# Forty-eight element-wise products of the delta rule's stage move from GpSimd's queue to VectorE's

## The reference, cut to what matters

```python
decay = jnp.exp(jnp.where(incl, gc[..., :, None] - gc[..., None, :], -jnp.inf))
kb = k * beta[..., None]
m = jnp.where(strict, jnp.einsum('bhnid,bhnjd->bhnij', kb, k) * decay, 0.0)
a_mat = m + jnp.eye(CHUNK, dtype=m.dtype)
sol = lax.linalg.triangular_solve(a_mat, rhs, left_side=True, lower=True, unit_diagonal=True)
...
v_new = u_n - jnp.einsum('bhlk,bhkv->bhlv', w_n, state)
state_next = state * jnp.exp(gl_n)[..., None, None] + jnp.einsum('bhlk,bhlv->bhkv', kd_n, v_new)
...
o = (jnp.einsum('bhnld,bhndv->bhnlv', q * jnp.exp(gc)[..., None], states)
     + jnp.einsum('bhnij,bhnjv->bhniv', attn, v_new))
```

## Time and profile before

| What | Value |
|---|---|
| median of the runs | 1362.28 us (3 runs, 1358.44 to 1362.96) |
| the profiled execution | 1358.39 us, span of its trace 1356.6 us |
| PE busy | 1221.3 us, 90% of the span |
| DVE busy | 814.8 us, 60% |
| POOL busy | 172.9 us, 13% |

### The profile page before, as it was taken

The page is one execution under the profiler, slowest core; times in us unless marked ns, Lnnn a source line. Parts: engine busy times, 40 slices in busy tenths (PEclk is TensorE's granted clock), DMA queues, the critical chain, the costliest instruction groups (busy, mean ns, idle before and its releaser), DMA issues.

```text
span 1356.6 us, 14615 instructions
## 1 busy us (share of the span) xinstructions
PE 1221.3 (90%) x5530; PEld 854.2 (63%) x5530; DVE 814.8 (60%) x1017; ACT 607.4 (45%) x777; POOL 172.9 (13%) x180
## 2 busy tenths in 40 slices
PE   4999999869999999898899399999999999999990
PEld 3788876556768778686468265566666666555540
DVE  7787841675344544426574576666666666666636
ACT  6353434633323324113231274566666666666632
POOL 1000250002313213220000001111111111111000
PEclk8999999979999999998899599999999999999995
DMA  6323321012122212201663899999999999999904
GB/s 237 94 87 114 110 62 38 10 32 75 43 63 57 76 40 62 73 21 55 212 241 119 325 321 333 351 397 407 400 401 402 393 395 392 401 401 396 380 8 189
DMA packets 96011, 278.55 MB, mean 205 GB/s; under 512 B 8768, under 2 KB 58560, under 8 KB 70720
## 3 DMA queue, kind: packets, MB, share of 16 engines
q1 hardware_dynamic: 90672, 268.63, 53.3%
q0 software_dynamic: 5120, 8.40, 1.9%
q10 hardware_dynamic: 144, 0.52, 0.1%
HBM read 267.04 MB, written 18.87 MB: 211 GB/s over the span
## 4 chain that ended last, share of the span: by engine, by line
PE 46%; DVE 2%; DMA 2%; issue 1%; ACT 1%; POOLq 0%; DVEq 0%; SPq 0%
PE yb L1792 17%; PE hb L1764 9%; PE hb L1765 9%; PE hb L1998 2%; PE tx L1748 2%; PE hb L1981 2%; PE gb L1779 1%; PE gb L1772 1%; PE yb L1998 1%; DMA h_dram<-h 1%; DMA xg<-h_dram,rows_all 1%; PE tx L2018 1%; PE yb L1981 1%; DVE yr L2342 0%; DVE h L2332 0%
## 5 line engine op out<-in xcount | busy, mean ns | idle before, releaser
L1881 DVE TENSOR_TENSOR wlo<-wraw,whi 128x2048 fp32r<-128x2048 f32 x127 | 285.4, 2287 | 29.3 <-ACT whi L1824 29.3
L1824 ACT ACTIVATE whi<-wraw 128x2048 fp32r<-128x2048 f32 x128 | 240.9, 1908 | 34.9 <-PE hb L1765 34.9
L1792 PE MATMUL yb<-wraw,act_t 128*64 128x512 f32 x512 | 230.8, 605 | 5.9 <-issue 5.9
L1764 PE MATMUL hb<-whi,xs 128*128 128x512 f32 x512 | 211.4, 413 | 1.7 <-DVE xs L1885 1.5
L1765 PE MATMUL hb<-wlo,xs 128*128 128x512 f32 x512 | 202.3, 395 | 0.0
L1184 PE MATMUL gate_ps<-h_part,gws 128*128 128x512 f32 x576 | 161.1, 420 | 3.3 <-ACT h L1334 3.1
L1792 PEld LDWEIGHTS yb<-wraw,act_t 128*64 128x64 f32 x512 | 68.5, 139 | 142.7 <-issue 140.9
L361 PE MATMUL pj<-h_part,wsplit 128*128 128x512 f32 x624 | 149.0, 397 | 0.0
L361 PEld LDWEIGHTS pj<-h_part,wsplit 128*128 128x128 f32 x624 | 116.8, 188 | 28.0 <-issue 3.4
L1184 PEld LDWEIGHTS gate_ps<-h_part,gws 128*128 128x128 f32 x576 | 105.7, 193 | 32.3 <-issue 12.7
L1764 PEld LDWEIGHTS hb<-whi,xs 128*128 128x128 f32 x512 | 97.4, 190 | 45.3 <-issue 27.3
(11 more groups left out here) (385 smaller groups left out, 1709.6 us busy)
## 6 DMA issues: line engine op xcount, KB each, us to landing
wraw<-in_moe_w SPq DMA_DIRECT2D x192, 1024.0 KB, 10.4
h<-in_w_in SPq DMA_DIRECT2D x24, 512.0 KB, 4.8
kTok<-in_w_in SPq DMA_DIRECT2D x6, 1024.0 KB, 5.6
vTok<-in_w_in SPq DMA_DIRECT2D x6, 1024.0 KB, 6.4
h<-in_w_in SPq DMA_DIRECT2D x4, 1024.0 KB, 5.5
h<-in_w_branch SPq DMA_DIRECT2D x16, 256.0 KB, 2.8
kept_dram<-h SPq DMA_DIRECT2D x16, 256.0 KB, 2.2
wraw<-in_w_out SPq DMA_DIRECT2D x2, 2048.0 KB, 12.1
```

The costliest lines, as they stand in the source:

```text
L1764: pe.matmul(bank[:, :], lhs, whi[:, u % NSPLIT, cols], start=(half == 0 and kk == 0), stop=False)
L1792: last = pe.matmul(yb[c][0:SLOTS, :], act_t[:, k, :], raw[:, room, cols], start=(k == 0), stop=(k == FT - 1))
L1824: act.activation(whi[:, u % NSPLIT, :], raw[:, room, :], ACT.Copy).then_inc(S.hi_done.sem, 1)
L1881: dve.tensor_tensor(wlo[:, u % NSPLIT, :], raw[:, room, :], whi[:, u % NSPLIT, :].bitcast(F32), ALU.subtract).then_inc(S.lo_done.sem, 1)
```

## The change

The 48 element-wise products that GpSimd made are made by DVE, each at a place in DVE's walk through the list: the product of q with the decays inside `gram`, behind line 1428 and ahead of the wait for ACT's exponential; the block mask at the end of `gram`, behind line 1436; the level's mask at the entry `y1`. GpSimd keeps the 32 clearings. The mask product of `y1` waits, as before, until the buffer of `ot` that it writes has been read by the `y1` two places earlier.

```diff
                     if kind == "gram":
...
                         dve.tensor_tensor(dd, dd, bc(cn("neg_fwd" if d == 0 else "neg_bwd"), 1, NH), ALU.add).then_inc(dif_ready, 1)
+                        q = qe[:, m % 4, :, :]
+                        dve.tensor_tensor(q, q, qkT[:, 0, :, tile(t)], ALU.mult).then_inc(qe_ready, 1)
                         dve.wait_ge(kk_done, m + 1)
                         dve.wait_ge(dec_ready, m + 1)
...
                         dve.tensor_tensor(mt[:, m % 4, :, :], mt[:, m % 4, :, :], bc(beta[:, t, col], 2, P), ALU.mult).then_inc(mt_ready, 1)
+                        dve.wait_ge(mt_ready, m + 1)
+                        dve.tensor_tensor(tt[:, m % 4, :, :], mt[:, m % 4, :, :], bc(cn("block"), 1, NH), ALU.mult).then_inc(masked, 1)
...
+                    elif kind == "y1":
+                        l = op[2]
+                        i = at_level(m, l)
+                        if i >= 2:
+                            dve.wait_ge(y1_done, i - 1)
+                        dve.tensor_tensor(ot[:, i % 2, :, :], mt[:, m % 4, :, :], bc(cn(f"level{d}_{LEVELS[l]}"), 1, NH),
+                                          ALU.mult).then_inc(ot_ready, 1)
...
-                    if kind == "gram":
-                        pool.wait_ge(egr_ready, m + 1)
-                        pool.tensor_tensor(qe[:, m % 4, :, :], qe[:, m % 4, :, :], qkT[:, 0, :, tile(t)], ALU.mult).then_inc(qe_ready, 1)
-                    elif kind == "attn":
-                        pool.wait_ge(mt_ready, m + 1)
-                        pool.tensor_tensor(tt[:, m % 4, :, :], mt[:, m % 4, :, :], bc(cn("block"), 1, NH), ALU.mult).then_inc(masked, 1)
-                    elif kind == "y1":
+                    if kind == "y1":
                         l = op[2]
                         i = at_level(m, l)
                         if i >= 2:
                             pool.wait_ge(p2_done, i - 1)
                         pool.memset(y1s[:, d, :, :], 0.0).then_inc(y1_cleared, 1)
-                        pool.wait_ge(mt_ready, m + 1)
-                        if i >= 2:
-                            pool.wait_ge(y1_done, i - 1)
-                        pool.tensor_tensor(ot[:, i % 2, :, :], mt[:, m % 4, :, :], bc(cn(f"level{d}_{LEVELS[l]}"), 1, NH),
-                                           ALU.mult).then_inc(ot_ready, 1)
```

## The result

The changed kernel takes 1393.09 us (median of 4 runs, 1391.64 to 1395.45) where the kernel before takes 1361.35 (4 runs): 1.0233 times as long, 95% interval 1.0218 to 1.0247, or 31.7 us more. The forecast was 1388, between 1376 and 1398.

What follows compares the result with a forecast made beforehand. TensorE was taken to bound the stage; waits 22.0 + 1.0 + 0.3 - 0.6 and clock 5.1 summed to 27.8 us, giving 1386.2 on the profiled execution, 1390.1 on the runs' median; named 1388, range 1376 to 1398.

Steps and rivals of the forecast that it cites:

- That TensorE bounds the stage and never waited for GpSimd: In the stage TensorE is busy 335.0 of 360.0 us; none of its waits is ended by GpSimd.
- The eight entries: Eight `y1` entries where TensorE arrives before DVE can make the mask: new waits of 1.5 to 4.4 us, together 22.0.
- The 0.5 us that `base` was to give back: Step after the second of the eight entries; itself waits for `spread`, so that entry counts 3.9 us, not 4.4.
- The small entries: Three other entries with DVE within a mask's length of TensorE: 0 to 2.1 us together, 1.0 taken.
- Inside `gram`: Block mask +0.7, q's product hidden, line 1428 gives back 0.45; only the first `spread` wait, for `facts`, counts: +0.3 us.
- What comes back: Weight split no longer slowed beside a GpSimd mask, so TensorE's 0.6 us wait for `tt` goes: -0.6 us.
- The clock: Stretches of 3.4 us at half clock after TensorE's new waits, 1.7 us lost each: three taken, 5.1 us; bounds 0 and 8.5.
- The sum: All terms over the stage: 22.0 + 1.0 + 0.3 - 0.6 + 5.1 = 27.8 us; later stages move by as much.
- load: Account stated with the experiments, not among the prediction's rivals: DVE simply has too much to do; no chance given.
- lateness: Fuller DVE late for `tt` updates, TensorE waits 0.7 us at each of 24 `again`, up to 16.8: 1403 us; 7 in 100.
- the port: DVE instructions slowed beside GpSimd's reads; freeing the port gives up to 9.1 us: 1349 us; 2 in 100.
- Half-absorbed: Half of the 25.0 us TensorE already waits in the stage takes in new lateness: sum 15.3, 1374 us; 1 in 10.

Runs made afterwards that it cites:

- the masks early: Change with all 48 products on DVE, but a level's two masks listed right behind the update by the level before: 1.0008 times the kernel before.
- The first experiment: Change with the 32 level masks back on GpSimd, the 16 products inside `gram` still on DVE: 1.0018 times the kernel before.
- the filled waits: Change plus needless matmuls in front of the five longest waits for a mask: 1387.15 us, 1.0181 times the kernel before.
- the unread masks: Kernel before plus 32 level masks on DVE that nobody waits for, at the change's places: 1.0001 times the kernel before.
- the run with four early pairs: Change with masks moved ahead only for the four `y1` pairs right behind a weight split: 1381.85 us, 1.0154 times the kernel before.

## Why the prediction was right

**That TensorE bounds the stage and never waited for GpSimd.** Right: taking GpSimd's products away, with the masks early, gave 1.0008.

**The eight entries.** Right in place, cause and size. The new idle time (bracket after, less bracket before) against the forecast, in order: 3.89 for 3.9, 4.38 for 4.4, 3.22 for 3.3, 1.97 for 2.0, 3.23 for 3.2, 1.49 for 1.5, 2.73 for 2.6, 1.53 for 1.6 us: together 22.4. Moving the masks without touching their number took the waits away; adding their number without the waits cost nothing. The 0.5 us that `base` was to give back fits too: its wait of 0.52 us was 0.10 in the changed trace. These are idle times of the weight load. The row of waits, 19.6 us, is that of the matmuls, and they idle less (3.49 us where the load of the first entry idles 3.93), because the matmul ahead still runs when the load falls idle. So the sum by loads is somewhat more than the stage lost by these waits.

**The small entries.** Two of the three waited, 0.67 and 0.37 us, together 1.0 as taken.

**Inside `gram`.** Right: q's product hid in the exponential's wait, line 1428 got its 0.45 us back, and the wait for `facts` grew by 0.2 us where 0.3 was taken. The first experiment shows the rest to be free.

**What comes back.** Right: the 0.6 us for `tt` is no longer among the waits.

**The clock.** The mis-sized term. I took three more slow stretches of 3.4 us, 5.1 us, and five as the bound, 8.5. Nine were there where the kernel before had three, six more: four of the five places are 6.8 us long, where I had priced 3.4. TensorE was busy for 28.4 of their 30.6 us, and in the three stretches of the kernel before for 10.2; half of each, as in the prediction, is 14.2 and 5.1. So the clock cost about 9.1 us more than before, an estimate from these rows, and a little above my bound. It is most of the 10.6 us by which TensorE was busy longer. The other 1.5 fit the start of `y1`: where it waits, its first matmul begins together with its weight load (both at 364.35), and before the change the load began 0.23 us earlier, under the matmul ahead (358.43 and 358.66). That the clock follows from the waits is shown by the filled waits, which took 5.7 us off the time in which TensorE does the same work; the rest of the 9.1 is read from the granted clock alone.

**The sum.** The stage grew by 30.0 us, where 27.8 were forecast. Without 9.1 for the clock 20.9 are left for everything else, where the forecast had 22.7. So the clock was taken 4.0 us too low and the rest 1.8 too high; that these errors partly cancelled is luck.

The rivals fell: load by the early and the unread masks, lateness by the early masks and by the absence of any wait at `again`, the port by the same early masks. Half-absorbed fell by the waits themselves, which came in full, and by the old ones, which did not shrink: without those for a mask TensorE idles 24.8 us in the stage, against 25.0 before. GPSIMD Engine Reference of the Trainium skill, Engine selection, is right on the product, 0.69 against 1.37 us; the kernel lost 2.3% by it all the same.

## What to carry to other kernels

An engine's queue is part of the price of an instruction: before moving work to a faster engine, look at what stands ahead of its new place, and whether that waits for the very engine which wants the result. The check needs only one trace: the end of the instruction listed ahead, plus the product, less the moment at which the consumer went through. If the result is positive, issue the work earlier in the queue, where its inputs are already there. The check prices the waits alone; here the lower clock behind them cost about 9 us more. And look for the same pattern in what the queue already holds: here that gave 7.4 us, where the choice of the engine by itself gave nothing.

## What the runs showed of the hardware that was not expected

Slow stretches of TensorE's clock do not follow a wait's length alone. The wait of 3.4 us for `rhs` brought one in the kernel before, in the run with four early pairs (588.4) and in the one with filled waits (590.0), but none in the changed kernel, whose 3.4 us after the same wait ran at full clock:

```profile
597.20:600.60 3.40, 3.40 (x25) 2.92 (x26) 1.81 (x3) 0.00 (x0) 0.52 (x1) 1.00 0.01 2
```

So when waits are taken away, slow stretches can turn up behind others, and a term for the clock keeps a wide bound.
